# A new order of the mixer's output projection, and six small edits beside it, in a two-stack transformer kernel

## The reference, cut to what matters

```python
for i in range(2):                                   # first stack
    x = layer_norm(ALPHA*x + 0.5*swiglu(x, ffn_w_in[i,0], ffn_w_out[i,0]))
    x = layer_norm(ALPHA*x + token_mix(x, mix_w_in[i], ..., mix_w_out[i]))
    x = layer_norm(ALPHA*x + 0.5*swiglu(x, ffn_w_in[i,1], ffn_w_out[i,1]))
    x = layer_norm(ALPHA*x + sigmoid(x @ w_gate + b) * (p[i] @ w_proj))
for l in range(2):                                   # second stack
    q_b, k_b = rotary(q_d), rotary(k_d)              # 16 of 64 channels are turned
    y_a, y_b = mla_attention(...), differential_attention(q_b, k_b, ...)
    x = layer_norm(ALPHA*x + (g_a*(y_a @ w_a) + g_b*(y_b @ w_b)) @ w_out)
```

## Time and profile before

| | us |
|---|---|
| median of 3 runs (1508.16 to 1509.04) | 1508.51 |
| the profiled execution | 1506.74 |
| its span, first to last instruction | 1504.9 |
| PE busy | 1490.7 |
| DVE busy | 943.8 |
| ACT busy | 816.1 |
| POOL busy | 217.7 |

### The profile page before, as it was taken

One profiled execution on the slowest core, in us unless ns is written; L12 is line 12 of the kernel. 1 busy time (PEld: TensorE's weight loads), 2 busy tenths in 40 slices (PEclk: granted clock), 3 DMA queues, 4 the chain that ended last, 5 costly groups with the idle time before them and its releaser, 6 DMA issues.

```text
span 1504.9 us, 27364 instructions
## 1 busy us (share of the span) xinstructions
PE 1490.7 (99%) x11622; PEld 1378.5 (92%) x11622; DVE 943.8 (63%) x1382; ACT 816.1 (54%) x1259; POOL 217.7 (14%) x127
## 2 busy tenths in 40 slices
PE   9999999999999999999999999999999999999998
PEld 8999899989998889998899989998789999899997
DVE  6655466676555475655557675655477767667756
ACT  6554366645454365554476554554375675555762
POOL 0000152113000261000432040000430001400001
PEclk9999999999999999999999999999999999999999
DMA  9655464326555456555553155555455334553341
GB/s 384 230 194 188 155 221 141 99 99 236 185 196 197 165 205 225 195 189 187 196 182 118 67 186 199 195 196 194 170 210 196 113 141 159 206 186 137 129 152 56
DMA packets 39720, 266.26 MB, mean 177 GB/s; under 512 B 4460, under 2 KB 4716, under 8 KB 9392
## 3 DMA queue, kind: packets, MB, share of 16 engines
q1 hardware_dynamic: 38304, 260.13, 49.1%
q0 software_dynamic: 720, 3.35, 0.6%
q10 hardware_dynamic: 576, 1.05, 0.2%
HBM read 263.46 MB, written 1.05 MB: 176 GB/s over the span
## 4 chain that ended last, share of the span: by engine, by line
PE 93%; DVE 4%; ACT 2%; issue 1%; DMA 0%; SPq 0%; ACTq 0%; DVEq 0%
PE PS L487 17%; PE PS L488 17%; PE PS L489 17%; PE PS L501 6%; PE PS L503 6%; PE PS L502 6%; PE PS L562 4%; PE PS L559 4%; PE PS L560 4%; PE PS L470 1%; PE PS L471 1%; PE PS L472 1%; PE PS L614 1%; PE PS L1954 1%; PE PS L1351 1%; PE PS L1968 1%
## 5 line engine op out<-in xcount | busy, mean ns | idle before, releaser
L487 PE MATMUL PS<-xTH,WH 128*128 128x256 f32 x2256 | 640.9, 284 | 0.0
L488 PE MATMUL PS<-xTL,WH 128*128 128x256 f32 x2256 | 628.3, 278 | 0.0
L489 PE MATMUL PS<-xTH,rawL 128*128 128x256 f32 x2256 | 626.3, 278 | 0.0
L319 DVE TENSOR_TENSOR rawL<-raw,WH 128x1024 fp32r<-128x1024 f32 (+1 forms) x408 | 491.5, 1231 | 112.9 <-ACT WH L316 112.4
L316 ACT ACTIVATE WH<-raw 128x1024 fp32r<-128x1024 f32 (+2 forms) x476 | 484.6, 1048 | 129.9 <-PE PS L562 101.3
L487 PEld LDWEIGHTS PS<-xTH,WH 128*128 128x128 f32 x2256 | 423.6, 188 | 9.0 <-issue 6.6
L488 PEld LDWEIGHTS PS<-xTL,WH 128*128 128x128 f32 x2256 | 423.7, 188 | 3.4 <-issue 2.9
L489 PEld LDWEIGHTS PS<-xTH,rawL 128*128 128x128 f32 x2256 | 424.7, 188 | 0.0
L319 POOL TENSOR_TENSOR rawL<-raw,WH 128x1024 fp32r<-128x1024 f32 (+1 forms) x68 | 162.5, 2413 | 766.4 <-ACT WH L316 766.4
L316 ACT ACTIVATE sg<-PS 128x256 f32<-128x256 f32 x79 | 30.4, 384 | 177.8 <-PE PS L489 177.8
L319 DVE TENSOR_TENSOR hh<-PS,sg 128x256 f32<-128x256 f32 x79 | 33.5, 424 | 144.9 <-ACT sg L316 144.9
(11 more groups left out here) (366 smaller groups left out, 2010.6 us busy)
## 6 DMA issues: line engine op xcount, KB each, us to landing
raw<-in_weights SPq DMA_DIRECT2D x233, 1024.0 KB, 4.8
gb<-in_lngb SPq DMA_DIRECT2D x16, 512.0 KB, 5.1
raw<-in_weights SPq DMA_DIRECT2D x2, 1056.0 KB, 4.9
gb<-in_ln SPq DMA_DIRECT2D x4, 512.0 KB, 4.4
cst<-in_consts POOLq DMA_DIRECT2D x1, 1378.5 KB, 10.3
x0T<-in_xT ACTq DMA_DIRECT2D x4, 256.0 KB, 5.7
raw<-in_weights SPq DMA_DIRECT2D x4, 256.0 KB, 5.3
xt<-in_x POOLq DMA_DIRECT2D x1, 1024.0 KB, 17.3
```

Of the source, the lines that this page charges most:

```text
L319: return Q.put(eng, waits, lambda e: e.tensor_tensor(out, a, b, op))
L487: e.matmul(out, c, xTH[:, k, :], start=k == 0, stop=False)
L488: e.matmul(out, c, xTL[:, k, :], start=False, stop=False)
L489: ins = e.matmul(out, u.L(i, 128 * k, 128), xTH[:, k, :], start=False, stop=k == KD - 1)
```

## The change

MIX_ORDER is changed, and the packing of the weights with it. One step of the stream moves ahead of the gram. In ln_apply the left half of the last norm goes over ScalarE and GpSimd, and the stores are reordered. The first chunk is rounded on VectorE. W' takes its products in another order, twelve in each part. sb_soft(1) goes ahead of rms(0) and rms(1). In rotary, w is of the rounded type and a low part wl is made from PSUM on VectorE; cos is applied to PSUM; the permutation is two products with a rounded copy of perm; the sin product has its own tile; va uses ring B.

```diff
-MIX_ORDER = [0, 1, 6, 7, 2, 3, 4, 5]
+MIX_ORDER = [0, 1, 2, 3, 6, 7, 4, 5]
@@ round_chunk
-        chunk_high[c] = act(WH[c % RING][:, 0:w], raw[n % RAW][:, o:o + w], ACT.Copy, [raw_loaded[n, i], free])
+        dst, src, waits = WH[c % RING][:, 0:w], raw[n % RAW][:, o:o + w], [raw_loaded[n, i], free]
+        chunk_high[c] = act(dst, src, ACT.Copy, waits) if c else copy(dst, src, waits)
@@ ln_apply(t, stats, eps, last=False)
+                if last and n == 0:
+                    c = stt(xt[:, t, cols], PS[:, b, 0:w], lnmv[:, t, 0:1], gb[:, 0, cols], ALU.subtract, ALU.mult, [a, gb_ready[0]])
+                    y = act(xt[:, t, cols], xt[:, t, cols], ACT.Copy, [r, c], scale=lnrs[:, t, :])
+                    done.append(tt(xt[:, t, cols], xt[:, t, cols], gb[:, 1, cols], ALU.add, [y], "pool"))
+                    continue
@@ end_phase, the last norm
-            x1 = ln_apply(1, stats, eps)
+            x1 = ln_apply(1, stats, eps, True)
+            store(1, 512, 256, x1[1][0])
             store(1, 0, 512, x1[0])
-            for part in range(2):
-                store(1, 512 + 256 * part, 256, x1[1][part])
+            store(1, 768, 256, x1[1][1])
@@ mix
         st["share"] = False
-        go(4)
+        go(5)
...
         next(v_conv[0])
-        go(3)
+        go(2)
...
-        tiles = [(i, [(1, 0), (1, 1)]) for i in range(4)] + [(i, [(0, 0), (1, 1), (0, 1), (1, 0)]) for i in range(4, 8)]
+        tiles = [t_ for i in range(4) for t_ in ((i + 4, (0, 0)), (i, (1, 1)), (i + 4, (0, 1)), (i, (1, 0)))]
+        tiles += [(i, (1, m)) for i in range(4, 8) for m in range(2)]
...
-        fill = [lambda: sb_scores(0), lambda: sb_scores(1), lambda: go(1), lambda: (go(1), sb_soft(1), sb_sums(0)), lambda: sb_sums(1),
+        fill = [lambda: sb_scores(0), lambda: sb_scores(1), lambda: go(1), lambda: (go(1), sb_sums(0)), lambda: sb_sums(1),
...
                 out_sum(c)
                 if c == 1:
+                    sb_soft(1)
                     rms(0)
                     rms(1)
@@ second, rotary
-            w = rw[i]
+            w, wl = rw[i], rl[i]
             a = act(w[:, :, :], v2(b), ACT.Copy, [p, rw_free[i]])
-            release(b, a)
-            c = tt(pr[:, :, :], w[:, :, :], two(C("dcos")), ALU.mult, [a, pr_free[0]])
+            lo = tt(wl[:, :, :], v2(b), w[:, :, :].bitcast(F32), ALU.subtract, [a])
+            c = tt(pr[:, :, :], v2(b), two(C("dcos")), ALU.mult, [p, pr_free[0]])
+            release(b, a, lo, c)
...
-                p2 = pe([a, free], lambda e: e.matmul(PS[:, b2, :], C("perm"), w[:, :, :].rearrange("p j s -> p (j s)"), start=True, stop=True))
-                s = tt(w[:, :, :], v2(b2), two(C("dsin")), ALU.mult, [p2, c])
+                    e.matmul(PS[:, b2, :], permR[:, :], w[:, :, :].rearrange("p j s -> p (j s)"), start=True, stop=False)
+                    return e.matmul(PS[:, b2, :], permR[:, :], wl[:, :, :].rearrange("p j s -> p (j s)"), start=False, stop=True)
+                p2 = pe([perm_ready, a, lo, free], fn)
+                s = tt(rs_[:, :, :], v2(b2), two(C("dsin")), ALU.mult, [p2, c])
...
-            b, free = bank("A")
+            b, free = bank("B")
```

More of the change, by code:

```diff
@@ L587, in ln_stats, with ln_apply @@
         return Q.put("dve", [y_tok], lambda e: e.bn_stats(out, src))
-    def ln_apply(t, stats, eps):
+    def ln_apply(t, stats, eps, last=False):
         table(TBL_SQRT)
@@ L1444, in mix @@
         wb = [bank("B") for _ in range(2)]
-        tiles = [(i, [(1, 0), (1, 1)]) for i in range(4)] + [(i, [(0, 0), (1, 1), (0, 1), (1, 0)]) for i in range(4, 8)]
+        tiles = [t_ for i in range(4) for t_ in ((i + 4, (0, 0)), (i, (1, 1)), (i + 4, (0, 1)), (i, (1, 0)))]
+        tiles += [(i, (1, m)) for i in range(4, 8) for m in range(2)]
         for part in range(2):
             def fn(e, part=part):
-                for i, quads in tiles[4 * part:4 * part + 4]:
-                    for a_, m in quads:
+                for i, (a_, m) in tiles[12 * part:12 * part + 12]:
                         R, M = slice(64 * a_, 64 * a_ + 64), slice(64 * m, 64 * m + 64)
@@ L1687, in second @@
         va = put_at("va", [128, 2, 512], 32)
-        rw = [put_at("rwa", [128, 2, S], 36), put_at("rwb", [128, 2, S], 38)]
+        rw = [put_at("rwa", [128, 2, S], 36, F32R), put_at("rwb", [128, 2, S], 38, F32R)]
+        rl = [put_at("rla", [128, 2, S], 70, F32R), put_at("rlb", [128, 2, S], 72, F32R)]
+        rs_, permR = put_at("rsum", [128, 2, S], 74), put_at("permR", [128, 128], 76, F32R)
         pr = put_at("pr", [128, 2, S], 40)
@@ L1754, in second @@
         xw = [xT_ready[0], xT_ready[1], par_ready]
+        perm_ready = act(permR[:, :], C("perm"), ACT.Copy, [xw])
         lp = PAR(l, "lam", 0, 256).rearrange("p (a b d) -> p a b d", a=2, b=2)
@@ L1797, in rotary, with fn @@
             rw_n[0] += 1
-            w = rw[i]
+            w, wl = rw[i], rl[i]
             a = act(w[:, :, :], v2(b), ACT.Copy, [p, rw_free[i]])
-            release(b, a)
-            c = tt(pr[:, :, :], w[:, :, :], two(C("dcos")), ALU.mult, [a, pr_free[0]])
+            lo = tt(wl[:, :, :], v2(b), w[:, :, :].bitcast(F32), ALU.subtract, [a])
+            c = tt(pr[:, :, :], v2(b), two(C("dcos")), ALU.mult, [p, pr_free[0]])
+            release(b, a, lo, c)
             def later():
                 b2, free = bank("B")
-                p2 = pe([a, free], lambda e: e.matmul(PS[:, b2, :], C("perm"), w[:, :, :].rearrange("p j s -> p (j s)"), start=True, stop=True))
-                s = tt(w[:, :, :], v2(b2), two(C("dsin")), ALU.mult, [p2, c])
+                def fn(e):
+                    e.matmul(PS[:, b2, :], permR[:, :], w[:, :, :].rearrange("p j s -> p (j s)"), start=True, stop=False)
+                    return e.matmul(PS[:, b2, :], permR[:, :], wl[:, :, :].rearrange("p j s -> p (j s)"), start=False, stop=True)
+                p2 = pe([perm_ready, a, lo, free], fn)
+                s = tt(rs_[:, :, :], v2(b2), two(C("dsin")), ALU.mult, [p2, c])
                 release(b2, s)
-                y = tt(dst, pr[:, :, :], w[:, :, :], ALU.add, [s, c])
+                y = tt(dst, pr[:, :, :], rs_[:, :, :], ALU.add, [s, c])
                 rw_free[i] = y
```

## The result

| | before | after |
|---|---|---|
| median of 6 runs each, us | 1508.81 (1508.16 to 1509.24) | 1504.42 (1502.91 to 1506.15) |
| the profiled execution | 1506.74 | 1502.91 |
| its span | 1504.9 | 1501.1 |
| DVE busy | 943.8 | 947.4 |

The ratio is 0.9972, 95% interval [0.9961, 0.9983]: 4.4 us faster by the medians, 3.8 by the spans. The forecast was 1503.4, from a sum of -5.05.

What follows compares the result with a forecast made beforehand. TensorE was taken as the bound. Terms -2.1 (projection), -0.65 (gram), -0.2 (sums), -1.8 (rotary), 0 (W'), 0 (first chunk), -0.3 (last norm) sum to -5.05; 1508.51 - 5.05 = 1503.4 us, 8-in-10 range 1501.6 to 1505.4.

Steps and rivals of the forecast that it cites:

- TensorE is the bound: Whole kernel: the chain lies on TensorE for 93%; an edit is worth what it takes out of TensorE's queue.
- The four edits there: Edits on TensorE: output projection -2.1, gram -0.65, sums -0.2, rotary -1.8 us.
- Output projection: Product order 0 1 2 3 6 7 4 5: the scL wait goes, gL is ready in time; gain 1.06 a layer, 2.1 in all.
- Gram: Half a tile moved ahead of the gram covers the wait before it; gain 0.33 us a layer, 0.65 in all.
- Sums: sb_soft(1) ahead of two norms: ez wait replaced by 0.35 us before the second head; gain 0.1 a layer, 0.2 in all.
- Rotary: Permutation as two rounded products: 0.40 won per rotary, 0.64 lost in a layer's first; gain 0.9 a layer, 1.8 in all.
- second: no wait: Second rotary of a layer: lo ends at 1144.2, TensorE arrives at 1144.27, so it does not wait.
- W': W' products by quadrant, 12 rotating, then 4 with the 8: taken as 0, bounds -0.3 to +0.4 us.
- First chunk: Rounded on VectorE at the start: first real product up to 0.8 us later, load sets the head; 0, bounds -0.1 and +0.5.
- Last norm: Left half over ScalarE and GpSimd, stores reordered, at the end: gain 0.35 or loss 0.15 us; taken as 0.3 gain.
- GpSimd's 1.29: Last norm: GpSimd's addition of 512 elements taken as 1.29 us, not the 1.80 also seen.
- the reason that I gave for it: Last norm: 1.80 ran beside VectorE passes with two SBUF inputs, sharing a port; 1.29 beside passes reading PSUM, as here.

Runs made afterwards that it cites:

- late pair: Kernel after, with the permutation products of the second rotary of a layer's first pair one chunk of the weight product later, between its halves: 1505.30, ratio 0.9978 to the kernel before.
- Moving the copy: Kernel after, with the step that brings the copy rsa issued ahead of the two norms of squares: 1503.15, ratio 0.9965 to the kernel before.
- half by ScalarE: Kernel after, with the store of the last norm's left half issued on ScalarE's queue: 1504.13, ratio 0.9970 to the kernel before.

## Why the prediction was right, and where its steps were not

*Right: TensorE is the bound, and an edit is worth what it takes out of its queue.* The four edits there were sized at 4.75 and gave 4.9 in the profiled pair, of which 2.6 is the order and came back in every trace. That the whole came within 1.0 of the forecast, by medians, is in part luck: the projection gave 0.44 more and the end 0.93 less than the sum has.

*Output projection: right in kind, too small.* The wait goes, the first k = 2 product starts 0.36 behind the transposes, k = 6 comes at 327.87, and gL ends at 331.61, 1.7 before the second pass. It gave 1.27 a layer, not 1.06. The term that was mis-sized: I took the idle time in brackets for the cost. From the transposes (324.89) to the product behind them were 1.65 us before, and are 0.36 now. The bracket counts from the modelled end of the last product (0.39 behind its start), which is later than the point at which a next one could start (0.23 behind it); and a product after a wait is followed at 0.31, not at 0.23. The distance of two starts has both. The order alone gave the same.

*Gram: right, but less.* 0.26 a layer for 0.33 at the first inverse step, and 0.14 of it is left by W' in the first mixer. Here I did the opposite, and took a distance of starts less a guess of 0.09 for the change of form.

*Sums: the mechanism right, the gain less still.* rsa in front of the second head, where I had counted it. But its cost, from 301.00 to 301.66 where 0.22 is normal, is 0.44 for the bracket's 0.27, and it eats the whole gain. Moving the copy showed it.

*Rotary: right in kind, the size not secure.* 0.79 and 1.02 for 0.9 in the profiled pair; alone the edit gave 1.3 in all for 1.8, by trace and medians. A pair costs 0.46 to 0.55, as worked out. The first pair waits for the residual, the third and fourth do not. In the second layer the waits' view names crs for the wait of 0.56; the timeline has rla ending at 1328.64 and the product at 1328.78, the same 0.14 behind the residual as in the first layer, so it is the residual there too. My "second: no wait" holds for the view, not for the queue: VectorE ends rlb at 1141.69, TensorE could have started at 1141.67 and starts at 1141.84. The late pair showed that no slack is left.

*W': 0, right. First chunk: 0, but of two parts that I did not have.* The half rate at the start costs up to 0.4 in five executions of eight, and a wait of 0.26 in the second mixer is gone. In the profiled execution after, the first did not show, and the second did. The row for the rounding of a chunk on VectorE, which the trace before lacked, now exists:

```profile
6.14 0.42 DVE L328 CAST WH<-raw 128x512 fp32r<-128x512 f32 x1
```

0.42, against 0.69 for the two-input pass of the same size. The Trainium skill (VectorE: DVE Perf Modes, The perf-mode tier table) gave it twice the rate; the trace has 1.6 times.

*Last norm: wrong in sign, -0.3 for +0.6.* GpSimd took 1.26, as chosen. ScalarE took 0.72 and not 0.64, so GpSimd was done 2.88 behind the start of the pass, not 2.75. The last two issues start 0.38 apart, so the last goes out 3.29 behind the start of the pass, where before it went at 3.48: 0.19 of the 0.35 is left. The step that failed is the next: the sum compares only the times at which the last store goes out, and so takes its landing to last as long as before. But before, three stores went out 0.92 apart, and now a half and a quarter are in flight together, 384 KB. From its issue the last quarter lands in 1.8 before, in 2.1 with the new last norm and no packet, in 2.6 to 3.0 with it. So the end comes 0.1 later than before without the packet of instructions, and 0.6 to 1.0 later with it. GpSimd's 1.29 was right; no run tested the reason that I gave for it.

*Not in the sum: the distance of products in unchanged code.* The kernel with only the new last norm is the same program as before up to 1499 us. Its products stand with the same offset to 1091 (0.05), and are 0.77 behind at 1134. One window of each, before first:

```profile
1119.39 0.28 PE L487 MATMUL PS<-xTH,WH 128*128 128x256 f32 x1
1119.50 0.28 PE L488 MATMUL PS<-xTL,WH 128*128 128x256 f32 x1
1119.62 0.28 PE L489 MATMUL PS<-xTH,rawL 128*128 128x256 f32 x1
1119.73 0.28 PE L487 MATMUL PS<-xTH,WH 128*128 128x256 f32 x1
```
```profile
1119.52 0.28 PE L487 MATMUL PS<-xTH,WH 128*128 128x256 f32 x1
1119.64 0.28 PE L488 MATMUL PS<-xTL,WH 128*128 128x256 f32 x1
1119.76 0.28 PE L489 MATMUL PS<-xTH,rawL 128*128 128x256 f32 x1
1119.88 0.28 PE L487 MATMUL PS<-xTH,WH 128*128 128x256 f32 x1
```

Three products take 0.34 in one and 0.36 in the other, at a granted clock of 1.00 (the level of 2.4 GHz) in both. By its last norm this kernel was 1.3 us behind the one before, with no edit at work. So single spans carry an error of over 1 us either way, the +0.73 in my table is of this kind, and the 1.3 by which span and forecast differ is no larger. Of the 14 traces only three have the shorter distance from 1109 to 1134 (before, gram and W' alone, half by ScalarE): it is the profiled execution before that was lucky there. What sets the level stays open.

## What to carry to other kernels

Read the price of a wait from the distance of two starts, with and without it; in the projection and in the sums the idle time in the brackets was 0.2 us short. Before a product is moved away from a wait, look at whether the engine that it waits for has idle time up to its next reader: if not, the wait moves with it. Before half a microsecond is booked to an edit, look at the same place in a second execution of both kernels. And at the end of a program count bytes in flight and look for every queue that moves something, since there nothing covers a transfer that lands late.

## What the runs showed of the hardware

- Products of 256 columns of the rounded type follow each other at 0.113 or at 0.118 to 0.120 us, for stretches of tens of us. The same instructions were at one level in one execution and at the other in another, at full granted clock.
- One 8 KB packet of the instruction queue among the last two stores went with an end 0.4 to 0.9 us later, in the 5 traces with the new last norm that had it; with the old last norm it was 0.3, in one trace.
- GpSimd's addition of 128 x 512 took 1.26 beside VectorE passes that read PSUM, in every trace with the new last norm.
- With the first product of the weights at 6.6 to 7.0 us, TensorE was at half rate (256 columns every 0.21 us) up to 10.3 to 11.3 us in 5 of 8 traces; with it at 6.1 to 6.2, in 0 of 6. In three of the five the granted clock reads 0.50.
- The last 128 KB store landed 1.8 us behind its issue with its neighbour 0.92 ahead of it, and 2.1 with 256 KB issued 0.38 ahead of it.
